# Forgetting attention: weight roundings between squares and root, the forget gate two slots later, five short passes for the q/k norms

## The reference

```
proj = x @ w_in                                   # 512 x 4112: q, k, v, g, f_logit
qh = rms_norm(heads(q)) * qn_g                    # 16 heads of 64
kh = rms_norm(heads(k)) * kn_g                    # x * rsqrt(mean(x*x) + 1e-6)
logf = log_sigmoid(f_logit + b_f)
c = cumsum(logf)                                  # over the 512 tokens, one row a head
s[t, s'] = qh_t . kh_s' / 8 + c_t - c_s'          # s' <= t
o = softmax(s) @ v * sigmoid(g);   return o @ w_out
```

## Time and profile before

| | |
|---|---|
| three timed runs | 1427.09, 1429.08, 3438.35 us |
| profiled execution | 1426.63 us |
| its span | 1424.8 us, mean granted TensorE clock 0.988 |
| TensorE matmul busy | 1352.9 us (95%) |
| GpSimd busy | 530.3 us (37%) |
| VectorE busy | 506.6 us (36%) |
| ScalarE busy | 492.9 us (35%) |
| DMA | 119.61 MB, mean 84 GB/s |

### The profile page before, as it was taken

How to read it: one execution, slowest core, us unless ns; L and a number is a source line. 1 busy time by engine, 2 the same in 40 slices (tenths; PEclk the granted TensorE clock), 3 DMA queues, 4 the chain that set the end, 5 groups by cost and what they waited for, 6 DMA issues and landing times.

```text
span 1424.8 us, 19060 instructions
## 1 busy us (share of the span) xinstructions
PE 1352.9 (95%) x7304; PEld 1124.4 (79%) x7304; DVE 506.6 (36%) x1057; ACT 492.9 (35%) x830; POOL 530.3 (37%) x421
## 2 busy tenths in 40 slices
PE   7999997789999999999998999999999999999997
PEld 7887875568888888888887788777788888888886
DVE  3366435646111111010763766654571111110005
ACT  4312326533322332221254655554333232232111
POOL 5422222042454444544144222222244445445440
PEclk9999998999999999999999999999999999999999
DMA  6211120022333332323123122212223333333231
GB/s 222 99 57 60 60 89 30 30 79 70 89 89 93 114 89 93 122 96 105 60 60 106 45 61 60 60 35 85 67 82 89 111 96 89 94 99 118 89 104 59
DMA packets 140233, 119.61 MB, mean 84 GB/s; under 512 B 5648, under 2 KB 118512, under 8 KB 140144
## 3 DMA queue, kind: packets, MB, share of 16 engines
q1 hardware_dynamic: 140144, 118.41, 26.5%
HBM read 116.20 MB, written 2.10 MB: 83 GB/s over the span
## 4 chain that ended last, share of the span: by engine, by line
PE 79%; DVE 9%; ACT 5%; issue 4%; POOL 1%; DMA 0%; ACTq 0%; DVEq 0%; SPq 0%; POOLq 0%
PE banks L471 24%; PE banks L473 24%; PE banks L472 24%; ACT w_hi L1038 1%; PE banks L750 1%; PE banks L863 1%; POOL w_lo L998 1%; PE banks L897 1%; PE banks L879 1%; ACT p_fox L1295 1%; DVE fox_ms L1579 1%; PE banks L542 1%; DVE x_res L1532 1%; PE banks L768 1%; DVE small L1494 1%
## 5 line engine op out<-in xcount | busy, mean ns | idle before, releaser
L998 POOL TENSOR_TENSOR w_lo<-w_raw,w_hi 128x512 fp32r<-128x512 f32 x417 | 530.1, 1304 | 862.6 <-ACT w_hi L1038 848.6
L471 PE MATMUL banks<-xT_lo,w_hi 128*128 128x512 f32 (+2 forms) x992 | 370.6, 374 | 2.2 <-DVEq L1337 1.6
L473 PE MATMUL banks<-xT_hi,w_hi 128*128 128x512 f32 (+2 forms) x992 | 367.4, 370 | 0.0
L472 PE MATMUL banks<-xT_hi,w_lo 128*128 128x512 f32 (+2 forms) x992 | 367.4, 370 | 0.0
L1038 ACT ACTIVATE w_hi<-w_raw 128x2048 fp32r<-128x2048 f32 (+1 forms) x107 | 200.0, 1869 | 192.2 <-PE banks L473 150.9
L471 PEld LDWEIGHTS banks<-xT_lo,w_hi 128*128 128x128 f32 (+1 forms) x992 | 185.4, 187 | 36.1 <-issue 4.9
L473 PEld LDWEIGHTS banks<-xT_hi,w_hi 128*128 128x128 f32 (+1 forms) x992 | 185.3, 187 | 32.8
L472 PEld LDWEIGHTS banks<-xT_hi,w_lo 128*128 128x128 f32 (+1 forms) x992 | 185.5, 187 | 31.2
L471 PE MATMUL banks<-w_lo,xT_hi 128*128 128x256 f32 (+1 forms) x544 | 185.5, 341 | 10.0 <-ACT q_raw L1060 3.3
L472 PE MATMUL banks<-w_hi,xT_lo 128*128 128x256 f32 (+1 forms) x544 | 179.5, 330 | 0.0
L473 PE MATMUL banks<-w_hi,xT_hi 128*128 128x256 f32 (+1 forms) x544 | 179.4, 330 | 0.0
(11 more groups left out here) (179 smaller groups left out, 1231.2 us busy)
## 6 DMA issues: line engine op xcount, KB each, us to landing
w_raw<-in_ffn_w_dram SPq DMA_DIRECT2D x92, 512.0 KB, 4.5
w_raw<-in_ffn_w_dram SPq DMA_DIRECT2D x20, 1024.0 KB, 4.8
w_raw<-in_fox_w_in_dram SPq DMA_DIRECT2D x16, 1024.0 KB, 5.8
w_raw<-in_even_w_in_dram SPq DMA_DIRECT2D x14, 1024.0 KB, 4.9
w_raw<-in_even_w_out_dram SPq DMA_DIRECT2D x4, 1024.0 KB, 4.9
w_raw<-in_fox_w_out_dram SPq DMA_DIRECT2D x4, 1024.0 KB, 4.8
x_res<-in_x_dram SPq DMA_DIRECT2D x4, 512.0 KB, 7.5
out_dram<-x_res SPq DMA_DIRECT2D x4, 512.0 KB, 2.6
```

What stands on the lines that cost most here:

```text
L471: mm(acc, l_hi, r_lo, start=first, stop=False)
L472: mm(acc, l_lo, r_hi, start=False, stop=False)
L473: return mm(acc, l_hi, r_hi, start=False, stop=final)
L998: ins = nc.gpsimd.tensor_tensor(w_lo[c % RING][:, a:a + n], w_raw[c % RAW][:, a:a + n], w_hi[c % RING][:, a:a + n].bitcast(F32), ALU.subtract)
```

## The change

It makes three edits in the mixer of layer 1.

The rounding of a coming chunk moves down in ScalarE's slot: it now stands after the copy and square of the q/k tile and after the copy of the turned tile, and before the root.

The forget gate's work moves from slots 8 and 9 to slots 10 and 11, on ScalarE and on VectorE. The place of the six DMAs in the SP queue's order stays as it was, ahead of the load of k1.

The norm of a q/k tile takes five VectorE passes instead of seven. The mean and the epsilon (L1579) go into the scale and bias of ScalarE's Ln, where the bias is read by pointer from a column that one new memset fills. The four passes of `refine` become three SCALAR_TENSOR_TENSOR of 128x4 that work from the sum of the squares. TENSOR_REDUCE and the multiply stay.

```diff
@@ ScalarE, root
-            def root(dst, src, arg_sem, n, done):
+            def root(dst, src, arg_sem, n, done, scale=1.0, bias=0.0):
                 act.wait_ge(arg_sem, n)
-                step(fn(dst, src, ACT.Ln))
+                step(fn(dst, src, ACT.Ln, scale=scale, bias=bias))
                 chain(fn(dst, dst, ACT.Exp, scale=-0.5), done)
@@ ScalarE, the loop over fox_steps
-                if piece and chunks[piece[0]][0] == "foxk0":
-                    if piece[1] % 2 == 0:
-                        hi_upto(piece[0] + 2 + piece[1] // 2)
-                elif piece and piece[1] == (3 if piece[0] == chunk_at("foxv0", 1) else 1):
-                    hi_upto(piece[0] + 3)
                 if values_at(i - 1):
...
                     chain(fn(sq[:, n % 2, :], q_raw[:, n % 2, :], ACT.Square), S["sq_done"])
                 if heads_at(i - 3):
                     turned_heads(*heads_at(i - 3))
+                if piece and chunks[piece[0]][0] == "foxk0":
+                    if piece[1] % 2 == 0:
+                        hi_upto(piece[0] + 2 + piece[1] // 2)
+                elif piece and piece[1] == (3 if piece[0] == chunk_at("foxv0", 1) else 1):
+                    hi_upto(piece[0] + 3)
                 if heads_at(i - 1):
-                    root(fox_ms[:, n % 2, 1, :], fox_ms[:, n % 2, 0, :], S["qvar"], n + 1, S["qroot"])
+                    n = heads_at(i - 1)[3]
+                    root(fox_ms[:, n % 2, 1, :], fox_ms[:, n % 2, 0, :], S["qsum"], n + 1, S["qroot"], 1.0 / HD,
+                         gains[:, 7:8])
...
-                if i == 2 * NT:
+                if i == 2 * NT + 2:
                     act.wait_ge(S["f_arg"], 1)
@@ VectorE, once at the start
+            step(v.memset(gains[:, 7:8], 1e-6))
@@ VectorE, square_sums
-                step(v.tensor_reduce(m[:, 0, :], sq[:, n % 2, :].rearrange("p (h d) -> p h d", h=4), AX_X, ALU.add))
-                chain(ts(m[:, 0, :], m[:, 0, :], 1.0 / HD, 1e-6, ALU.mult, ALU.add), S["qvar"])
+                chain(v.tensor_reduce(m[:, 0, :], sq[:, n % 2, :].rearrange("p (h d) -> p h d", h=4), AX_X, ALU.add),
+                      S["qsum"])
@@ VectorE, fox_heads
-                refine(m[:, 1, :], m[:, 0, :], m[:, 2, :])
+                total, r, tmp = m[:, 0, :], m[:, 1, :], m[:, 2, :]
+                step(stt(tmp, r, -0.5 / HD, r, ALU.mult, ALU.mult))
+                step(stt(tmp, total, HD * 1e-6, tmp, ALU.add, ALU.mult))
+                step(stt(r, tmp, 1.5, r, ALU.add, ALU.mult))
@@ VectorE, the loop over fox_steps
-                if i == 2 * NT:
+                if i == 2 * NT + 2:
...
-                if i == 2 * NT + 1:
+                if i == 2 * NT + 3:
                     dve.wait_ge(S["f_ln"], 1)
```

More of the change, by code:

```diff
@@ L262, in build @@
               "exp_done", "mix_done", "pT_done", "lam_arg", "lam_exp", "f_arg", "f_ln", "logf_done",
-              "sq_done", "qvar", "qroot", "qn_done", "qk_done", "v_done", "g_done", "act_free", "gated",
+              "sq_done", "qsum", "qroot", "qn_done", "qk_done", "v_done", "g_done", "act_free", "gated",
               "fmax", "fexp", "fnorm", "fpT_a", "fpT_b", "c_split", "c_in", "o_gated", "o_hi", "o_lo")
```

## The result

The changed kernel took 1432.68 us (median of 11 runs, 1430.43 to 1435.82), the kernel before 1428.27 (median of 11: 1425.9 to 1430.31, and one of 3438.35). The ratio of the times without that one is 1.0036 [1.0028, 1.0044]: 4 to 5 us slower, where 2 to 4 us faster were forecast. The median lies above the stated range, 1415 to 1431. Within 2% it is no change, as forecast; the sign was missed.

A forecast was written before the change was run, and what follows sets the result against it. TensorE was taken to bound the stage, busy 267.47 of its 285 us, with 18.6 us at most to be had. 1426.63 + 0.2 (memset) - 0.5 (to the first scores) - 1.5 (attention steps) = 1424.8 us; range 1415 to 1431.

The forecast's parts named there:

- Turnings 3 and 5: Opening, turned q/k tiles: passes held in GpSimd's moved bursts make these turnings start 1.9 and 2.6 us later.
- Rival A: Norm passes: the new passes do not wait in bursts, or meet few; 1413 to 1418 us, chance 0.2.
- Turning 7: Opening: waits only for the products, so it starts at 749.7 instead of 752.48, 2.8 us earlier.
- The 5.00: TensorE's 5.00 us wait in the opening, behind ScalarE's forget-gate work and a rounding; expected to go.
- two steps of 2.9 us: From turning 5 to turning 7: each step is 12 matmuls of 0.22 and a turning.
- To the first scores: Opening up to the first scores: between -0.7 and +0.8 us, taken as -0.5.
- 757.4 to 758.9: Forget gate: when c_parts are split, against 753.66 before; the six copies and k1's load follow.
- near the early end, since the gate's passes meet only the burst's tail: Forget gate's VectorE passes: the reason for taking -0.5 us from the span -0.7 to +0.8.
- rival B: First scores: k1's load decides, gate's scan and a pass held by GpSimd; scores +1.9, 1430 us, chance 0.2.
- The attention steps: The 32 attention steps: -6.3 of waits gone, +4.8 from later bursts, -1.5 us; bounds -6.3 and +1.5.
- with L1579 gone ScalarE is earlier: Attention steps: ScalarE's late copies of probabilities come earlier, so 3.0 us of L849's waits are credited whole.
- 34.9 down to under 12: ScalarE's waits for the norms' sums: 34.9 us in total, expected to fall to under 12.

The follow-up runs named there:

- the pair with roundings in the middle: Changed kernel with roundings behind the square, ahead of the turned copy: 1427.89 us; the same with k1's load ahead of the six c_parts copies: 1423.91 us.
- the filler: Changed kernel plus junk transposes ahead of turnings 3, 5, 28 and the first scores: 1438.13 us; at turning 3 alone 1433.57, at the first scores alone 1433.95.

## Why the prediction was wrong, by its own steps

The forecast had the stage 2.0 us shorter (-0.5 and -1.5); in the profile it is 5.5 longer. Of these 7.5 us, 3.1 arise up to the first scores and 4.4 in the attention steps.

**Turnings 3 and 5: right.** +1.9 and +2.6 forecast, +1.88 and +2.66 measured, by the mechanism named. Rival A is out: the form with a plain number waits as well, 0.71, 1.22 and 1.20 us.

The Trainium skill (SBUF — State Buffer, SBUF: two separate sides) has GpSimd and a VectorE pass with two SBUF inputs exclude each other for a whole instruction. The rows agree: 0.16 outside a burst, 1.22 in it.

**Turning 7: half right.** The 5.00 and its slow clock went, but -0.9 came for -2.8. The step that failed is "two steps of 2.9 us": from turning 5 to turning 7 it took 7.61 us, and 3.40 us of that ran at 0.50. In the five kernels with five passes or fewer and the clock up there (roundings first or in the middle, no refining) the same stretch takes 5.97 to 6.03. The forecast counted the slow clock that would go and left out the one that its own new waits would bring: none lay behind the 1.33 that turning 5 waited before, one lay behind its 2.08.

**To the first scores: forecast -0.5, measured +2.6.** The mechanism is the one worked out in the forecast: copies, k1's load, its rounding, the last v tile, the scores; ScalarE waited 6.89 for the load, TensorE 4.73. The sizes were off. The split comes at 760.3 in the time of the kernel before (764.22 less 3.9), late of "757.4 to 758.9". Against the early end, 757.4, that is 2.9 us: 2.0 because the gate's Exp starts at 752.6 and not 750.6, behind the late turning 7, and 0.9 because one pass of the split met the tail of GpSimd's burst:

```profile
760.56 1.34 DVE L1626 TENSOR_SCALAR c_parts<-gate_T 16x512 bf16<-16x512 f32 x1
```

The same pass took 0.41 before (L1620), so "five passes, 2.8 outside" took 3.7 again. The step that failed is "near the early end, since the gate's passes meet only the burst's tail". This is near rival B: it names 758.2 as the point from which the load decides and 760 for the split, and +1.9 for the scores. One of its two causes came, the held pass; the scan took 1.21, as before, and the rest was the slow clock, which B does not have. That a scan can be held too, the kernel with roundings first shows: 2.07.

**The attention steps: forecast -1.5, measured +2.9,** beyond the bounds (-6.3 to +1.5). Here the mechanism was wrong too. Up to turning 27 the account roughly held: from +2.56 at the first scores to +2.3 at turning 26 and +1.0 at turning 27. Then turning 28 waits 3.48 instead of 1.25 and stands at +3.6, and turning 29 is at +6.0, the last steps at +5.5. The 3.0 us on late probabilities that the forecast "credited whole" doubled to 6.1. The failed step is "with L1579 gone ScalarE is earlier": the sum has one pass less before it only outside bursts, and in a burst it stands behind three passes and a multiply. "34.9 down to under 12" failed for the same reason, with 33.8. The experiment without passes shows it (6.3, and no wait at turning 28), and that with roundings first too (24.7, and 0.64 there). The 2.4 us between turnings 28 and 29 are the half clock, as the pair with roundings in the middle shows (5.81 and 3.40 behind waits alike). The forecast has no term for it.

**The clock as a whole.** Of four slow stretches two cost nothing, as the filler shows: what follows turning 3 or the first scores waits for another engine soon anyway. The 1.9 ahead of turning 7 and the 2.4 behind turning 28 are where TensorE leads. Filler at turning 5 did not keep its stretch fast (0.64 from 748 to 752 us), and that at turning 28 did not get ahead of the wait, so both rest on comparisons between kernels. Why the clock fell behind one wait and not behind another as long stays open.

**Small terms.** Ln with a pointer took 0.30 for 0.20, just above the bound of 0.09 more. The gate's Exp, load and Ln follow each other within 0.03 us, as before. The drain that the Trainium skill (ScalarE: Activation LUTs, What ACT_TABLE_LOAD costs) adds to a switch is not in these rows either. The 3.3 us of L471 went, as forecast (0.4 left). The memset was not looked at by itself.

**Chances.** 0.98 for within 2% was right, with all the idle time at 18.6 us. Rival B's side was the right one, and B had 0.2 where the forecast had 0.5; but its 1430 falls short of 1432.68 as well, since it took +1.5 for the steps that came at +2.9. The forecast's own margin at the load was 0.8 us and that of its turnings nil, so any further lateness went straight to B's side.

## What to carry to other kernels

An instruction that is moved past a few short ones also moves the burst it sets off on another engine: list what that engine's neighbours do in the new place, including what stands *behind* them in order for the next tile. Before an edit frees an engine, follow the freed time to the next thing that waits in a queue; here a load behind six small copies took it all back, and moving it ahead gave 0.32 to 0.46%, as much as the best of the three edits. Count the slow clock that the new waits bring as well as the one that goes, but only where TensorE is what the next step waits for. Two edits that are each worth nothing or a gain by themselves can cost together: the late gate did so only with the late roundings.

## What the runs showed of the hardware that was not expected

- The multiply of 128x256 takes 0.42 to 0.43 us alone and 0.70 to 1.58 beside GpSimd's instructions of 1.25 (the change and the kernel without refining), while the TENSOR_REDUCE of as many elements takes 0.42 in both. In a burst each pass of a row ends with a GpSimd instruction, so 0.5 us of three passes became 3.1.
- The clock fell to the lower level behind waits of about 2.1 us (738.9 and 749.1), and did not behind the 1.12 and 0.91 of the kernel with roundings first. But no length of wait decides it in these rows: ahead of turning 3 a wait of 2.31 us stands in two kernels (roundings alone; seven passes with late roundings and late gate), and behind it the clock fell in the first and not in the second. Behind 2.6 us at turning 28 it was the same.
- A faster clock between two waits moved no end: 1.5 us won behind turning 3 came back as 1.5 us more at turning 5.
